# Two raw weight units at the head of the second block, a second set of transposes for the normalised activations, and the first output products beside the last attention head

## The reference, cut to what matters

```python
def first_block(...):
    ...
    h = h + hier_moe(rms_norm(h, norm2_g[l]), ...)
    return rms_norm(h, norm_f_g)

def hybrid_layer(x, ln1, w_in, b_f, sinks, w_pa, w_pb, w_pc, w_o, ...):
    h = rmsnorm(x, ln1)
    z = h @ w_in
    qa, ka, va, qb, kb, vb, fb, qc, kc, vc, ga, gb, gc = jnp.split(z, points, axis=-1)
    o_a = moba_attention(heads(qa, A_HEADS), heads(ka, A_HEADS), heads(va, A_HEADS), tbl_a)
    o_b = forgetting_attention(heads(qb, B_HEADS), heads(kb, B_HEADS), heads(vb, B_HEADS), fb + b_f)
    o_c = sliding_window_sink_attention(heads(qc, C_HEADS), heads(kc, C_KV_HEADS), heads(vc, C_KV_HEADS), sinks, tbl_c)
    merged = (jax.nn.sigmoid(ga) * (o_a @ w_pa)
              + jax.nn.sigmoid(gb) * (o_b @ w_pb)
              + jax.nn.sigmoid(gc) * (o_c @ w_pc))
    x = x + merged @ w_o
    ... # norm, feed-forward with a short convolution, final norm
```

## Time and profile before

| | us |
|---|---|
| three runs | 975.77, 976.76, 979.15; median 976.76 |
| profiled execution, its own time | 979.41 |
| its span | 977.7 |
| PE busy | 864.1 (88%) |
| DVE, ACT, POOL busy | 503.9, 388.2, 81.2 |
| mean granted clock of PE | 0.947 |

### The profile page before, as it was taken

One profiled execution on the slowest core, in us unless ns is written; L12 is line 12 of the kernel. 1 busy time (PEld: TensorE's weight loads), 2 busy tenths in 40 slices (PEclk: granted clock), 3 DMA queues, 4 the chain that ended last, 5 costly groups with the idle time before them and its releaser, 6 DMA issues.

```text
span 977.7 us, 14771 instructions
## 1 busy us (share of the span) xinstructions
PE 864.1 (88%) x5993; PEld 717.1 (73%) x5993; DVE 503.9 (52%) x781; ACT 388.2 (40%) x523; POOL 81.2 (8%) x105
## 2 busy tenths in 40 slices
PE   4899998999996876686669699999989999999996
PEld 4899798999984433333123598998878799999995
DVE  5798567645565211111001744545557557666674
ACT  5333535454332111110112544545553356656462
POOL 1132001120000000000000001111134000000000
PEclk9999999899999898998779799999989999999998
DMA  6755463244769599999997856242532927564711
GB/s 206 259 184 189 156 223 123 87 173 164 306 240 422 235 423 422 422 421 422 422 421 281 175 147 195 90 173 87 152 107 89 296 77 250 178 208 147 239 45 43
DMA packets 93875, 217.50 MB, mean 222 GB/s; under 512 B 16455, under 2 KB 43973, under 8 KB 81537
## 3 DMA queue, kind: packets, MB, share of 16 engines
q1 hardware_dynamic: 93137, 215.32, 60.8%
q10 hardware_dynamic: 576, 1.18, 0.3%
q0 software_dynamic: 112, 0.30, 0.3%
HBM read 215.44 MB, written 1.34 MB: 222 GB/s over the span
## 4 chain that ended last, share of the span: by engine, by line
PE 66%; DMA 16%; DVE 10%; ACT 4%; issue 3%; SPq 1%; POOL 0%; DVEq 0%; ACTq 0%
PE ps L748 15%; PE ps L749 15%; PE ps L750 15%; DMA moe_ring<-in_w_expert_in 13%; PE ps L1051 6%; PE ps L985 5%; DVE w_lo L1414 3%; ACT w_hi L1136 1%; DMA stage<-in_w_in 1%; PE ps L910 1%; PE ps L964 1%; PE ps L895 1%; DMA stage_b<-in_w_up 1%; SPq L619 1%; PE ps L946 1%
## 5 line engine op out<-in xcount | busy, mean ns | idle before, releaser
L748 PE MATMUL ps<-x_hi,w_hi 128*128 128x256 f32 x1008 | 291.3, 289 | 7.0 <-DVE w_lo L1414 4.9
L749 PE MATMUL ps<-x_lo,w_hi 128*128 128x256 f32 x1008 | 288.0, 286 | 0.0
L750 PE MATMUL ps<-x_hi,w_lo 128*128 128x256 f32 x1008 | 287.9, 286 | 0.0
L748 PEld LDWEIGHTS ps<-x_hi,w_hi 128*128 128x128 f32 x1008 | 196.4, 195 | 10.0 <-DVE w_lo L1414 6.3
L749 PEld LDWEIGHTS ps<-x_lo,w_hi 128*128 128x128 f32 x1008 | 196.3, 195 | 0.3
L750 PEld LDWEIGHTS ps<-x_hi,w_lo 128*128 128x128 f32 x1008 | 196.0, 194 | 0.0
L1414 DVE TENSOR_TENSOR w_lo<-stage,w_hi 128x2048 fp32r<-128x2048 f32 (+2 forms) x72 | 162.1, 2291 | 56.4 <-ACT w_hi L1136 54.7
L1136 ACT ACTIVATE w_hi<-stage 128x2048 fp32r<-128x2048 f32 (+2 forms) x74 | 133.1, 1849 | 67.4 <-PE ps L750 59.8
L985 PE MATMUL ps<-moe_ring,qk 128*32 128x512 f32 x384 | 56.6, 745 | 41.8 <-DMA moe_ring<-in_w_expert_in 41.8
L985 PEld LDWEIGHTS ps<-moe_ring,qk 128*32 128x32 f32 x384 | 13.5, 132 | 81.0 <-DMA moe_ring<-in_w_expert_in 47.3
L748 PE MATMUL ps<-w_hi,x_hi 128*128 128x512 f32 (+2 forms) x176 | 65.9, 374 | 3.6 <-DVE x_lo L1421 1.9
(11 more groups left out here) (310 smaller groups left out, 1475.4 us busy)
## 6 DMA issues: line engine op xcount, KB each, us to landing
stage<-in_w_in SPq DMA_DIRECT2D x24, 2048.0 KB, 7.8
moe_ring<-in_w_expert_in SPq DMA_DIRECT2D x48, 1024.0 KB, 17.3
moe_ring<-in_w_expert_out SPq DMA_DIRECT2D x16, 1024.0 KB, 21.1
stage_b<-in_w_up SPq DMA_DIRECT2D x12, 1024.0 KB, 8.1
stage<-in_w_down SPq DMA_DIRECT2D x11, 1024.0 KB, 5.1
stage<-in_w_up SPq DMA_DIRECT2D x10, 1024.0 KB, 9.3
up_odd<-in_w_expert_in SPq DMA_DIRECT2D x8, 1024.0 KB, 18.6
down_odd_a<-in_w_expert_out SPq DMA_DIRECT2D x8, 1024.0 KB, 21.2
```

The costliest lines, as they stand in the source:

```text
L748: mm(out, still[0], moving[0], start=first, stop=False)
L749: mm(out, still[0], moving[1], start=False, stop=False)
L750: return mm(out, still[1], moving[0], start=False, stop=last)
```

## The change: what it does

1. The first unit of the second block is `vvf` (A values, C values, forget logits, 388 columns). It is loaded to a place of its own (`first_stage`) as soon as the seventh of the eight quads has left `y_slots`, and POOL does both parts of its split (a cast, L2038, and a subtraction, L2041, for each half) during the last quad.
2. The scatter's matmuls go by token tile instead of by half, so that tile 0 is complete earlier (semaphore `scat0`); DVE scales each tile as it comes.
3. PE transposes `h_tok` itself, without either norm's factor; ACT and DVE make `raw_hi` and `raw_lo` from it. `vvf` (2 fills of 24 matmuls with 388 moving columns) and `qka` (2 fills of 48) are computed from these raw activations.
4. The factors are worked out meanwhile. They are applied afterwards: to the values and forget logits on the way out of PSUM (`rstd2`), to the A queries in the logits' scale (`scale_q`), to the A keys by a row `r_row` that PE makes in step `rrow`.
5. DVE scales `xs_tok` as before; its 16 transposes are now the steps `xn` 0 to 3 in banks 4 to 7, between the two fills of `qka`, for `x_hi` and `x_lo` of all later units.
6. `kbvb` moves ahead of the heads; the last unit there is `qbkc`, whose C keys stand ahead of head 0 and whose B queries are the fill of head 0. That leaves 15 fills for heads 0 to 14. Head 15 gets `pab` 0 to 3, and `pab` 4 to 7 stand between its `pt` and its `av`.
7. Slots of the weight parts change (`ff_pair`) so that both units of the start find free memory.

The list and the new pieces (of helpers and evacuations those that carry the change):

```diff
     steps.append({"op": "moe"})
-    steps.append({"op": "between"})
-    steps.append({"op": "norm", "i": 2})
     units_one = len(units)
-    steps.extend(unit("kvc", 0, [0, 1], 2))
+    for half in range(2):
+        steps.append({"op": "split", "unit": units_one, "half": half})
+    for half in range(2):
+        steps.append({"op": "split", "unit": units_one + 1, "half": half})
+    steps.append({"op": "norm", "i": 2})
+    steps.append({"op": "between"})
+    steps.extend(unit("vvf", 0, [0, 1], 3))
+    fills = unit("qka", 0, [0, 1])
+    steps.append(fills[0])
+    at("rrow")
+    for b in range(4):
+        at("xn", b)
+    steps.append({"op": "rescale"})
+    steps.append(fills[1])
+    fills = unit("kbvb", 0, [0, 1])
+    steps.append(fills[0])
     at("cum")
+    steps.append(fills[1])
     for h in range(HEADS_B):
         at("cumrow", h)
-    steps.extend(unit("qka", 0, [0, 1]))
-    steps.extend(unit("vaqb", 0, [0, 1]))
-    gates = unit("kbvb", 0, [0, 1]) + unit("qc", 0, [0, 1], 2 * KT)
+    fills = unit("qbkc", 0, [1, 0], 2)
+    steps.append(fills[0])
+    gates = fills[1:] + unit("qc", 0, [0, 1], 2 * KT)
...
+    gates = [gates[n:n + 1] for n in range(heads - 1)]
+    fills = unit("pab", 0, range(8), 2)
+    gates += [fills[0:4], fills[4:8]]
...
# PE, quad: the scatter
-                for half in range(2):
-                    eng.wait_ge((y_a, y_b)[half], it + 2)
-                    for t in range(NT):
+                for t in range(NT):
+                    for half in range(2):
+                        if t == 0:
+                            eng.wait_ge((y_a, y_b)[half], it + 2)
...
-                last.then_inc(scattered, 1)
+                    last.then_inc((scat0, scattered)[t], 1)
# PE, fill_at
+                elif kind == "rrow":
+                    eng.wait_ge(rstd2_ready, 1)
+                    for t in range(NT):
+                        last = mm(ps[:, bank, t * P:(t + 1) * P], rstd2[:, t:t + 1].broadcast_to([P, P]), ident[:, :], ...)
+                elif kind == "xn":
+                    for t in range(NT):
+                        eng.wait_ge(xn_ready, t + 1)
...
# ACT, in place of squares_of_psum and between
+            def between(t):
+                eng.wait_ge(scaled, t + 1)
+                act(junk[:, t, :], ps[...], ACT.Square, accum_out=ss[:, t:t + 1]).then_inc(squares, 1)
+                eng.wait_ge(squares, 5 + t)
+                act(junk[:, t, :], h_tok[:, t, :], ACT.Square, accum_out=ss_g[:, t:t + 1]).then_inc(squares_g, 1)
# DVE, end of moe
+                eng.wait_ge(scat0, passes * QUADS)
+                tt(h_tok[:, 0, :], ps[:, 4:6, :]..., wide_g[:, :], ALU.mult).then_inc(scaled, 1)
+                eng.wait_ge(scattered, passes * QUADS + 1)
+                tt(h_tok[:, 1, :], ps[:, 6:8, :]..., wide_g[:, :], ALU.mult).then_inc(scaled, 1)
# POOL
+                    if n == units_one:
+                        eng.wait_ge(first_in, 16 * 3)
+                        step(eng.tensor_copy(hi[:, cols], staged(n)[:, cols]))
```

More of the change, by code:

```diff
@@ L48 @@
 FFN_UNITS = FFN_TILES // 2
+WIDTH = {"kiwi": P, "vvf": 388, "qbkc": 384}
 WINDOW = 128
@@ L190, in schedule @@
             at("pt", HEADS + h - 1)
-        if h < heads and gates:
-            steps.append(gates.pop(0))
+        steps.extend(gates[h])
         if h >= 1:
             at("av", HEADS + h - 1)
-    assert not gates
-    steps.extend(unit("pab", 0, range(8), 2))
     steps.extend(unit("pc", 0, range(4), 2))
@@ L206, in schedule @@
     for s in steps:
-        if s["op"] == "norm" and s["i"] == 2:
-            spread_out += [{"op": "split", "unit": units_one, "half": half} for half in range(2)]
-        n = s.get("unit")
-        if n is not None and n + 1 not in (units_one, len(units)):
+        n = s.get("unit") if s["op"] == "pj" else None
+        if n is not None and n + 1 not in (units_one, units_one + 1, len(units)):
             if s["first"]:
@@ L784, in fill_pj @@
                         coming.append((k, lambda k=k: eng.wait_ge(dve_split, (4 if kind == "wo" else 8) + k // 2 + 1)))
+                if kind == "kbvb" and i == 0:
+                    for k in range(0, KT, 2):
+                        coming.append((k, lambda k=k: wait_read(eng, "at", "xn", k // 2)))
                 coming.sort(key=lambda c: c[0])
@@ L807, in fill_pj @@
                 elif kind in ("qi", "q", "k", "su", "ga", "gb", "g2", "qka", "qc"):
+                    x = (raw_hi, raw_lo) if kind == "qka" else (x_hi, x_lo)
                     for m in range(2):
-                        last = by_features(bank, m * S, w, ((i % 2) * 2 + m) * P)
+                        last = by_features(bank, m * S, w, ((i % 2) * 2 + m) * P, x=x)
                 elif kind in ("v", "sv"):
@@ L1145, in evac_pj @@
                 two = src.rearrange("p (m t) -> p m t", m=2)
-                if kind in ("v", "sv", "su", "ga", "gb", "g2", "kvc", "qka", "vaqb", "kbvb", "qc") and not (kind == "kvc" and i == 0):
+                if kind in ("v", "sv", "su", "ga", "gb", "g2", "kbvb", "qbkc", "qc") or (kind, i) == ("qka", 0):
                     eng.wait_ge(pj_full, n + 1)
@@ L1194, in evac_at @@
                     act(lp[:, i % 2, :], src[:, 0:384], ACT.Relu).then_inc(free, 1)
+                elif kind == "xn":
+                    eng.wait_ge(at_full, n + 1)
+                    for m in range(2):
+                        k = 2 * i + m
+                        act(x_hi[:, k, :], src[:, m * S:(m + 1) * S], ACT.Copy, scale=vec[:, C_LN1 + k:C_LN1 + k + 1]).then_inc(xn_hi, 1)
+                elif kind == "rrow":
+                    eng.wait_ge(at_full, n + 1)
+                    act(r_row[:, :], src[:, 0:S], ACT.Copy).then_inc(free, 1)
                 elif kind == "sguw":
@@ L1335, in _ @@
                         router()
[L1336 removed]
+                    if s["kind"] == "qka" and s["i"] == 1:
                         log_sigmoid()
@@ L1726, in evac_at @@
                     eng.sem_inc(rinv_ready, 1)
+                elif kind == "xn":
+                    eng.wait_ge(xn_hi, 2 * i + 2)
+                    for m in range(2):
+                        k = 2 * i + m
+                        last = stt(x_lo[:, k, :], src[:, m * S:(m + 1) * S], vec[:, C_LN1 + k:C_LN1 + k + 1], x_hi[:, k, :].bitcast(fp32),
+                                   ALU.mult, ALU.subtract)
+                    last.then_inc(free, 1)
                 elif kind == "cum":
@@ L1909, in _ @@
                     ffn()
+                elif s["op"] == "rescale":
+                    rescale()
                 elif s["op"] == "between":
+                    for half in range(2):
+                        split(units_one + 1, half)
                     between_norm()
```

221 lines of the change are left out of this document (130 added, 91 removed).

## The result

The changed kernel takes 963.42 us (median of four runs, 960.62 to 964.24) against 977.27 before: a ratio of 0.985, with a 95% interval of 0.9832 to 0.9867. That is 13.9 us less. Forecast were 957.1 us, a gain of 19.7, in a range from 953.5 to 965.5; the measured median is in the range, but outside the 954.5 to 959.5 that I gave a chance of 0.60. Five further runs of the changed kernel gave 962.39 against 977.25, ratio 0.9832 (0.9812 to 0.9852), 14.9 us less.

What follows compares the result with a forecast made beforehand. PE was taken as the bound, losing time in pauses and a halved clock at the boundary and heads' end. 9.9 + 9.5 + 1.1 - 0.8 = 19.7 us gave 959.7 profiled, 957.1 median; range 953.5 to 965.5.

Steps and rivals of the forecast that it cites:

- The boundary: From the last scatter to head 0: raw activations let PE start early and fill its pauses, gain 9.9 us.
- the collision: Ahead of tile 0's scaling: DVE's SBUF-only rank update waits while POOL works on SBUF, cost 0.8 us.
- the bound of 2.6: Upper limit for the wait of DVE's rank update: one POOL instruction less the 1.1 us until tile 0 is complete.
- POOL's split: Two casts and two subtractions for `vvf` ahead of the boundary: 12.3 to 18.7 us, hidden at cost 0, otherwise 1.5.
- (a) to (c): DVE work to be hidden at the boundary: factors by 555.5, `qka` parts by 552, scalings, evacuations, `kbvb` split, `x_lo` by 566.6.
- The heads: Heads 0 to 14 keep their form, 48 matmuls each, so head 15 starts 9.9 us earlier.
- (a) to (d): All that must be hidden at the boundary: DVE's factors, splits, scalings, evacuations and `x_lo`, plus SP's weight loads up to `qbkc`.
- The last head: From head 15 to the end of `pc`: 28.7 us instead of 38.25, gain 9.5, with pauses of 1.25 and 1.2.
- Behind `pc`: After `pc`: ACT begins the `wo2` split earlier, so PE's 1.85 us idle shrinks, gain 1.1, ends 0 and 1.85.
- (1): Rival at the boundary: the clock falls all the same, `vvf` and `qka` 0 at half clock, price 5.1, 962.2 us; chance 0.13.
- (3): Rival at POOL: late by its load or its casts, price 3 us, 960.1 us; chance 0.14, a third beyond 962.

Runs made afterwards that it cites:

- the run with POOL out of it: Changed kernel with the `vvf` weight parts made by ACT and DVE, POOL doing nothing there: 963.19 us, ratio 0.9832.
- The run with the `qc` split moved: Changed kernel with DVE's subtraction of the `qc` split put behind head 0's softmax instead of ahead of its logits: 964.12 us, ratio 0.9855.
- The long pause alone: Changed kernel with five more DVE multiplications ahead of the scaling of tile 0, so PE stands still longer behind the last scatter: 967.45 us.
- the late execution: Profiled execution, 965.19 us, of the changed kernel with both halves of the `wo2` split on DVE; POOL started 5.8 us ahead of the scatter instead of 6.95.
- the boundary alone: Changed kernel with the end of the heads as before, the `pab` fills behind the last `av`: 966.52 us, ratio 0.9895.
- the `wo2` split: Changed kernel with both halves of the `wo2` split on DVE, none on POOL: 960.49 us, ratio 0.9805.

## Why the prediction was right, and where its sizes were off

The sign and the places held; the gain was 13.9 us where 19.7 were forecast, so the median is in the range thanks to the room left for the rivals. By its steps, in the profiled executions:

- **The boundary**, 9.9 less 0.8 for L1806: measured 8.35 (57.05 to 48.70). `vvf` started 8.70 us behind the scatter's start where I had 7.38 without the collision. The 1.3 between them come from the wait for POOL: L1879 at 2.37 us delays the scaling of tile 0 by 1.5, and ACT's squares and `raw_hi` with it. This is read from the timeline; the run with POOL out of it shows only 0.5 of it (`vvf` at 8.19), since DVE then has a split of its own in the way. I had 0.8; the bound of 2.6 was well placed. `vvf` itself took 8.55 instead of 8.2, and from there to head 0 31.45 against 31.6.
- **POOL's split** took 9.9 us, not 12.3 to 18.7. A cast of 1552 columns is 1.48 us, under both of my rows. The cover (a) to (c) held: no wait at 559 or in `kbvb` 0.
- **The heads** were to keep their form. They became 1.2 us longer, of which 1.01 is a wait of `pt` 0 for POOL's probabilities: DVE has the `qc` split ahead of head 0's logits. I had counted (a) to (d) of what is late, but not this queue. The run with the `qc` split moved confirms the order as the cause of the delay, but not a way to get the 1.0 back.
- **The last head**, 9.5: measured 38.25 - 29.3 = 8.95, with pauses of 1.15 and 1.34 where I had 1.25 and 1.2. `pab` 4 starts 9.57 us behind `qk` 15, as forecast; the other 0.6 is spread over `pab` 4 to 7 (5.94 for 5.7), `av` 15 and its parts (2.20 for 2.0) and `pc` (11.58 for 11.4).
- **Behind `pc`**, 1.1: measured 1.85 - 0.78 = 1.07.

The stages sum to 17.4 instead of 19.7. The step that failed is "The heads 0 to 14 keep their form" (1.2); next come the last head (0.6), the collision's cost, 1.3 where I took 0.8, and `vvf`'s matmuls, interpolated too low (0.35).

Of the signs that I named, two were off: the first `vvf` matmul started 5.0 us behind the end of the last scatter (540.08 to 545.05) and not within 4, and `pc` ended at 733.2 and not near 731. In the first trace of the changed kernel the others held.

The medians give 2.2 to 3.5 us less gain than the stages. One cause is shown to exist: the execution in which POOL was 1.1 us later against the scatter lost 2.7 at the boundary, which is rivals (1) and (3) together, by the collision and not by PE's wait for the weights. It appeared in one of the eight traces that have this code (the other seven: update 2.09 to 2.49 us). How often it happens in runs without a trace, and whether it makes up the whole difference, stays open, as does the spread ahead of the last scatter. The mean granted clock doesn't settle it: in the first set it is 0.960 at 960.62 us and 0.955 to 0.958 in the three slower executions, but the second trace has 0.958 too, with nothing slow at the boundary.

**The clock.** I had read the 0.50 behind the boundary as the price of the one pause behind the scatter. The long pause alone cost 6.6 us for 6.4 us of added pause. In the traces with 7.3 us or more and then 1.7 to 4.0, the work behind was slow; in the one with 7.3 and 0.71 it wasn't; but behind 2.10 and 0.92 in the late execution `vvf` ran its first 3.4 us at 0.50 too. In the heads and at the norm single pauses of 2.46, 2.12 (twice), 2.28 and 1.90 us were each followed by a stretch at 0.50 of about 3.4 us, and one of 1.84 was not. So the change does take the slow stretch at the boundary away, as forecast, in five of the six traces with this boundary and no added pause, but a rule by the length of pauses alone doesn't cover head 15 (3.1 us of pauses with 0.50 before and 1.00 with the boundary alone), and I have none that does.

**The lock.** The Trainium skill ("SBUF — State Buffer", Who interferes with whom) speaks of an exclusive lock between VectorE and GpSimd. The traces agree: the update took 2.37 for 0.18, the addition 4.16 for 0.69, POOL's multiplication 4.88 for 0.61, and each ends 0.05 to 0.6 us behind the other engine's instruction. With POOL out of the way both DVE operations were back at 0.18 and 0.69. Not every DVE operation is held up: L1591, which reads PSUM, took 0.69 at 725.02, beside the same POOL split that held up the addition. In the prediction I gave a one-input operation the low end; it takes the wait in full. Of the Trainium skill's other sentence ("GPSIMD Engine Reference", Instruction dispatch), about 6 us for the first call of a freshly loaded kernel, nothing shows here: the last part of the load is issued at 520.75 and lands 8.6 us later, the first cast starts at 529.40 and takes 1.48 us, as the second does, and no gap follows. Whether any code had to be loaded for it these runs don't show.

## What to carry to other kernels

An instruction moved to GpSimd can be paid for by VectorE where both work on SBUF at the same time, and the other way round: look at what the other engine runs in those microseconds, small operations above all, before counting the move as free. Removing the pauses of one place was worth nothing here while the next one was bound by another engine; the wait turned up behind `pc` and then at the norm, and of the edits there only the one at that engine (the `wo2` split) gained, 0.4 to 0.6 us in its stage. When a slow clock is read as the price of a pause, lengthen the pause in the new kernel before believing it.
